# Two edits to a two-network kernel: the first expert's down tiles go through the counted loop, and the gate rows of the dense down stages are made one by one

## The reference, cut to what matters

```python
def moe_swiglu(h, w_router, w_gate, w_up, w_down):      # 8 experts, top 2, EXPERT_DIM 3584
    ...
    for e in range(N_EXPERTS):
        y = swiglu(h, w_gate[e], w_up[e], w_down[e])    # (silu(h@w_gate) * (h@w_up)) @ w_down
        out = out + gates[..., e:e + 1].astype(h.dtype) * y

# second network, D_FF 2816, two layers; the first has ctx and lat tokens, the last has lat only
        lat = lat + g2 * conv_ffn(modulate(rms_norm_2(lat, norm2_g[i]), sh2, sc2),
                                  ffn_w_up[i], ffn_conv_w[i], ffn_w_down[i])
        if not last:
            ...
            cx = cx + cg2 * conv_ffn(...)
```

## Time and profile before

| | before |
|---|---|
| runs, us | 2849.44, 2859.58, 2862.84 (median 2859.58) |
| profiled execution: its own time, span | 2855.28 us, 2853.5 us |
| instructions | 73493 |
| TensorE busy with matmuls | 2650.5 us, 93% of the span |
| VectorE, ScalarE, GpSimd busy | 899.9, 416.7, 86.5 us |
| mean granted clock of TensorE | 0.975 |
| ring transfers | 555 of 1024 KB, median 7.9 us from issue to landing |
| matmuls of the up and of the down tiles | 508.0 and 256.8 us |
| matmuls of the dense down stages | 266.1 us |

### The profile page before, as it was taken

The page is one execution under the profiler, slowest core; times in us unless marked ns, Lnnn a source line. Parts: engine busy times, 40 slices in busy tenths (PEclk is TensorE's granted clock), DMA queues, the critical chain, the costliest instruction groups (busy, mean ns, idle before and its releaser), DMA issues. The chain is left out here.

```text
span 2853.5 us, 73493 instructions
## 1 busy us (share of the span) xinstructions
PE 2650.5 (93%) x32426; PEld 2080.3 (73%) x32426; DVE 899.9 (32%) x2013; ACT 416.7 (15%) x1077; POOL 86.5 (3%) x131
## 2 busy tenths in 40 slices
PE   8979998988899999999998898989999999898998
PEld 4848847668899899899897446875888644455983
DVE  1120061121001001001002324653555675233776
ACT  2010001011000000000001211221222200131330
POOL 0000000000000000000000002210000000000000
PEclk9989999999999999999998999999999999999999
DMA  6964436539999999999992111001222244302441
GB/s 263 359 280 148 148 133 251 218 122 348 366 404 421 411 416 420 413 397 422 406 416 87 45 59 45 3 2 59 75 88 89 74 162 163 117 15 74 158 154 74
DMA packets 81706, 592.56 MB, mean 208 GB/s; under 512 B 9056, under 2 KB 9184, under 8 KB 10336
## 3 DMA queue, kind: packets, MB, share of 16 engines
q1 hardware_dynamic: 81360, 589.51, 52.3%
q10 hardware_dynamic: 144, 0.07, 0.0%
HBM read 588.50 MB, written 1.05 MB: 207 GB/s over the span
## 5 line engine op out<-in xcount | busy, mean ns | idle before, releaser
L1857 PE MATMUL ps<-arena,ring 128*64 128x80 f32 x14336 | 508.0, 233 | 30.9 <-issue 27.6
L1857 PEld LDWEIGHTS ps<-arena,ring 128*64 128x64 f32 x14336 | 501.7, 137 | 36.5 <-issue 33.7
L1866 PE MATMUL ps<-arena,ring 128*64 128x80 f32 x7168 | 256.8, 234 | 19.4 <-issue 19.4
L1866 PEld LDWEIGHTS ps<-arena,ring 128*64 128x64 f32 x7168 | 252.3, 138 | 22.8 <-issue 22.4
L1126 PE MATMUL ps<-ring,arena 128*128 128x512 f32 x616 | 266.1, 593 | 0.0
L1126 PEld LDWEIGHTS ps<-ring,arena 128*128 128x128 f32 x616 | 116.5, 190 | 146.0 <-issue 143.0
L2007 DVE TENSOR_TENSOR arena<-arena,ps 128x80 f32<-128x80 f32 x224 | 53.3, 238 | 479.2 <-ACT arena L1986 479.2
L3229 PE MATMUL ps<-hT,ring 128*128 128x256 f32 (+1 forms) x1056 | 182.6, 330 | 4.1 <-ACT par L3356 2.1
L3229 PEld LDWEIGHTS ps<-hT,ring 128*128 128x128 f32 x1056 | 162.6, 193 | 18.9 <-DVE hT L479 2.2
L1986 ACT ACTIVATE arena<-ps 128x80 f32<-128x80 f32 x224 | 53.2, 238 | 773.1 <-PE ps L1857 773.0
L1010 PE MATMUL ps<-hT,ring 128*128 128x256 f32 (+1 forms) x736 | 152.7, 370 | 2.7 <-ACT hT L482 2.7
(11 more groups left out here) (526 smaller groups left out, 2899.2 us busy)
## 6 DMA issues: line engine op xcount, KB each, us to landing
ring<-in_stream SPq DMA_DIRECT2D x555, 1024.0 KB, 7.9
par<-in_params SPq DMA_DIRECT2D x1, 3397.0 KB, 16.3
h<-in_x SPq DMA_DIRECT2D x2, 512.0 KB, 4.2
cx<-in_ctx SPq DMA_DIRECT2D x2, 512.0 KB, 18.0
out<-h SPq DMA_DIRECT2D x4, 256.0 KB, 2.0
par<-in_params SPq DMA_DIRECT2D x1, 873.0 KB, 6.2
par<-in_params ACTq DMA_DIRECT2D x1, 68.0 KB, 4.0
```

Source lines behind the costliest of these rows:

```text
L1857: last = nc.tensor.matmul(ps[m:m + 64, up_bank[j], half * P:half * P + CAP], w[:, k, half * P + m:half * P + m + 64], hTe[:, k, :], start= ...
L1866: last = nc.tensor.matmul(ps[m:m + 64, 6 + q // 4, (q % 4) * P:(q % 4) * P + CAP], w[:, j, q * P + m:q * P + m + 64], hid[:, 2 * d + j, :] ...
```

## The change

Two edits. In the expert loop the written-out down tiles of the first expert are gone. All eight experts use the loop of two turns; GpSimd copies blocks for expert 0 too, and the constants in the waits are one higher. In the dense down stage `gate_rows_now` is replaced by `gate_row(n)`, which makes one chunk. It is called in the second group of the first pass, behind m1, m2, m3 and m5 for chunks 0 to 3, always in bank 5. The diagonals stay where they were on VectorE.

```diff
-            def gate_rows_now(diag_known):
+            def gate_row(n):
+                (st, q), b = chunks[n], 5
+
                 @block.tensor
                 def _(pe):
                     pe.wait_ge(dve_done.sem, diag_known)
-                    for n, b in zip(range(len(chunks)), (5, 3, 1, 4)):
-                        claim(pe, b)
-                        last = nc.tensor.matmul(ps[:, b, :], ones, scr[n], start=True, stop=True)
-                    pe_done.by(last)
+                    claim(pe, b)
+                    pe_done.by(nc.tensor.matmul(ps[:, b, :], ones, scr[n], start=True, stop=True))
 
                 @block.scalar
                 def _(act):
                     act.wait_ge(pe_done.sem, pe_done.n)
-                    for (st, q), b in zip(chunks, (5, 3, 1, 4)):
-                        act_done.by(nc.scalar.activation(rows[:, st, q * 512:q * 512 + 512], ps[:, b, :], ACT.Copy))
-                        freed[b] = [(act_done, act_done.n)]
+                    act_done.by(nc.scalar.activation(rows[:, st, q * 512:q * 512 + 512], ps[:, b, :], ACT.Copy))
+                freed[b] = [(act_done, act_done.n)]
...
+                    some_rows = gate and p == 0 and gi == 1
                     product("m1", p, gi)
+                    if some_rows and len(chunks) > 0:
+                        gate_row(0)
                     for i in tiles:
                         weight_sum("t1", p, i)
-                    diag_known = gate_diagonals(layer, which, streams, scr) if p == gi == 0 and gate else 0
+                    if gate and p == gi == 0:
+                        diag_known = gate_diagonals(layer, which, streams, scr)
                     product("m2", p, gi)
+                    if some_rows and len(chunks) > 1:
+                        gate_row(1)
                     for i in tiles:
                         weight_sum("t3", p, i)
-                    if diag_known:
-                        gate_rows_now(diag_known)
...
                     product("m3", p, gi)
+                    if some_rows and len(chunks) > 2:
+                        gate_row(2)
...
                     product("m5", p, gi)
+                    if some_rows and len(chunks) > 3:
+                        gate_row(3)
...
-                for d in range(2 * kd if e == 0 else 0):
-                    pe.wait_ge(landed[slot(nf + d)], wait_of(nf + d))
-                    down_products(ring[:, slot(nf + d), :].rearrange("p (k n) -> p k n", k=2), d)
-                if e:
-                    with pe.Fori(0, 2) as part:
-                        for d in range(kd):
-
-                            pe.wait_ge(landed[slot(nf + d)], part * 16 + (16 * (per // RING) * e + wait_of(nf + d)))
-                            pe.wait_ge(moe_moved[d], part + e)
-                            down_products(ring[:, slot(nf + d), :].rearrange("p (k n) -> p k n", k=2), d)
+                with pe.Fori(0, 2) as part:
+                    for d in range(kd):
+
+                        pe.wait_ge(landed[slot(nf + d)], part * 16 + (16 * (per // RING) * e + wait_of(nf + d)))
+                        pe.wait_ge(moe_moved[d], part + (e + 1))
+                        down_products(ring[:, slot(nf + d), :].rearrange("p (k n) -> p k n", k=2), d)
...
             for d in range(kd):
                 pool.sem_inc(moe_moved[d], 1)
-            for e in range(1, EXPERTS):
+            for e in range(EXPERTS):
                 hid_made(pool, e * nf + nf - 1)
```

## The result

The changed kernel took 2840.35 us (median of 7 runs, 2833.9 to 2843.91), the kernel before 2857.16 us beside it (7 runs, 2849.44 to 2865.77). The ratio is 0.9939, 95% interval [0.9921, 0.9956]: 17 us faster, where 15.3 were predicted, with 2842 us as the time. The profiled execution took 2843.64 us, span 2841.8 us.

What follows compares the result with a forecast made beforehand. TensorE, busy 93% of the span, was taken as the bound, with DMA close beside it in the experts. Gains of 4.9 + 7.1 + 3.3 = 15.3 us gave 2842 us, own range 2836 to 2848, with the others 2833 to 2854.

Steps and rivals of the forecast that it cites:

- The first expert's second seven tiles, 3.9 us: First expert's down tiles: three gaps of fresh code go when the second seven repeat the first's code; 3.9 us gained.
- The second expert's up tiles, 1.5 us between 0.3 and 2.7: Second expert's first up tiles, behind the new loop: code brought in while it repeats; 0.3 to 2.7 us gained, 1.5 taken.
- DMA allows it, 0.5 us off: Expert loops: DMA can supply the faster tiles, but room is short further on, so 0.5 us is taken off.
- The room of 7.8 us: First 62.6 us window: its 22.7 MB need 54.8 us at 415 GB/s, leaving 7.8 us for a 5.4 us gain.
- The branch of the prediction that spoke of moved code borders: Rival, behind 1500 us: moved work and code borders could lengthen low-clock stretches; 2863 us in its example, chance 0.05.
- The term of the first edit: Expert loop: 3.9 + 1.5 - 0.5 = 4.9 us gained, ends 0 and 6.6.
- The first gated stage, 7.1 us: First gated down stage: 6.58 + 6.29 us before against 2.35 + 3.44 after; 7.1 us gained, ends 4.2 and 7.6.
- The step on the clock: First gated stage: clock stays up over 2.35 us of idle time; if it fell, 2.9 us would be given back.
- The last stage, 3.3 us: Last down stage: 5.17 us before against 1.9 us after; 3.3 us gained, ends 2.5 and 3.5.
- DMA fell: Rival, expert loops: DMA takes the first edit's gain; 10.4 us remain, 2846.5 us, chance 0.14.
- The branch's fetch: Rival, first expert's down loop: the branch back costs a fetch, gaps return; 9.2 us remain, 2847.5 us, chance 0.07.
- Slower by the clock: Rival, whole kernel: TensorE's clock falls behind small waits, low stretches grow; 2863 us with 42 us more, chance 0.05.

Runs made afterwards that it cites:

- the run at a DMA share of 0.70: Changed kernel with half of each expert weight tile transferred, TensorE's instructions the same and the experts' results wrong; 2781.63 us (one run).

## Why the prediction was right

- *The first expert's second seven tiles, 3.9 us*: the two profiles of before and after give 19.46 - 15.61 = 3.85 us; with the other profiles of that code (18.91) it is 3.3. Right, and the mechanism is shown from both sides: written out eight times it costs 3.5 us in the first expert and 4.3 on the mean in the others, and with the DMA at 0.70 the fresh first turns of the same place have no gap.
- *The second expert's up tiles, 1.5 us between 0.3 and 2.7*: 20.49 - 20.23 = 0.26 us; as means of four profiles of either expert code 20.5 and 20.2, where the old code's four lie between 19.1 and 22.0, so no gain is shown at all. The size was wrong, at or below the low end of its bounds. I read two later experts' first turns, 2.1 and 4.5 us over, as what a loop ahead gives; the table of turns shows that such turns differ by 2 us and more with the place of the block borders, and by up to 1.4 us between two executions.
- *DMA allows it, 0.5 us off*: nothing had to come off. Waits of more than 0.1 us for tiles that had just landed were 0 to 1.3 us in all in four profiles with the old expert code and 0.1 to 0.4 in four with the new. The room of 7.8 us, from the 363 GB/s of the earlier trace rows, was the right reading.
- *Missing from the sum*: the code behind the edit. Over experts 1 to 7 the first down turns were 6 to 7.5 us shorter and the first up turns 3 to 4 us longer in the two pairs of profiles; with the other turns it is 3.5 us net in the profiled pair. The branch of the prediction that spoke of moved code borders put them among the losses, far behind. The term of the first edit was 4.9 us and measured 7.0 (8.7 as the mean of four profiles of each expert code). That 4.9 came as near as it did is partly luck: of its three parts one held, the other two measured about nothing, and 3 us that it did not have came from behind.
- *The first gated stage, 7.1 us*: 6.7. The step on the clock was right (no fall over the wait; it was 2.45 us, not 2.35), m7 did not wait on t3, and rows and products took the forecast 0.43 us an instruction.
- *The last stage, 3.3 us*: 3.0, with a wait of 0.28 us where 0.2 was forecast.
- *The rivals*: DMA fell. The branch's fetch fell: not one of the eight loops has a gap in its second turn (15.49 to 15.61 us). The Trainium skill's section "Instruction fetch mechanics" ("Runtime: NRT & Kernel Launch") gives TensorE's instruction memory as 2,048 instructions and, in its warning against taken branches, a window of two pages, by its blocks of 256 instructions 512; the prediction used one word for both. A body of 896 instructions fits the first and not the second, and it repeats without a gap, so for this body the trace agrees with the first; no run here varied the size of the body. The section's sentence that crossing a block border is mostly hidden agrees with the run at a DMA share of 0.70 and not with those at 0.94 to 1.0, where fresh code costs some 1.2 us a block (4.3 us for three and a half). Slower by the clock did not happen, but its size is real: 124 and 144 us at the low level in two executions of one kernel.

The sum was low by 2.1 us in the experts and high by 0.7 in the stages (0.4 and 0.3), 1.4 us low in all by the profiled pair; the time of 2842 us came out within 2 us of the median.

## What to carry to other kernels

Where TensorE goes through an instruction every 17 ns (34.9 for a matmul and its load) beside full DMA engines, fetching code costs time: a loop of repeated tiles can be worth its extra copies and waits. Gaps marked "issue" at equal counts of instructions, each some 2.4 us behind the start of a packet in the instruction queue, are the sign. A wait that two or three independent products could cover is best removed by moving the waiting instruction behind them, and where the clock falls in the wait, that cost goes too. When an edit changes the length of the code, compare the whole stretch behind it and not single turns, since the borders of the blocks move and with them the turns that have the gaps.

## What was not expected of the hardware

- With the same instructions, gaps of 1.2 us on the mean for a block of 256 at a DMA share of 0.94 to 1.0, and at 0.66 to 0.72 nearly none: 2.5 us in all over seven experts, for 38.5.
- A written-out stretch makes the code behind it slower too: first up turns 146.5 us for 140.3 when the down tiles ahead of them are written out, although these first turns are fresh in both. The traces show 25 blocks fetched during these turns for 22.
- The place of the borders moves single turns by about 2 us or more, 17.7 to 18.4 against 20.4 to 20.6 us for the same seven tiles in two profiles of each kernel, and leaves the sum over tiles 141 to 448 as it was within 1.4 us.
